# Both branch projections as seven products per block, with their operands and their merge passed through DRAM

## The reference

```
merged = jax.nn.sigmoid(ga_raw) * jnp.einsum('bne,ed->bnd', y_a, w_pa) + jax.nn.sigmoid(gb_raw) * jnp.einsum('bne,ed->bnd', y_b, w_pb)
return jnp.einsum('bnd,de->bne', merged, w_out)
```

## Time and profile before

| | |
|---|---|
| median of 3 runs | 1795.55 us (1794.21 to 1795.87) |
| the profiled execution's own time | 1793.51 us |
| its span, first to last instruction | 1791.8 us |
| PE busy | 98% |
| DVE busy | 59% |
| ACT busy | 34% |
| granted PE clock, mean | 0.996 of full speed |
| gate stage | from 692.0 to 844.4 us |
| branch stage | to 1018.5 us |
| output stage, first half of its columns | to 1064.8 us |

### The profile page before, as it was taken

How to read it: one execution, slowest core, us unless ns; L and a number is a source line. 1 busy time by engine, 2 the same in 40 slices (tenths; PEclk the granted TensorE clock), 3 DMA queues, 4 the chain that set the end, 5 groups by cost and what they waited for, 6 DMA issues and landing times.

```text
span 1791.8 us, 22991 instructions
## 1 busy us (share of the span) xinstructions
PE 1751.6 (98%) x8577; PEld 1471.9 (82%) x8577; DVE 1062.6 (59%) x1587; ACT 602.0 (34%) x937; POOL 169.2 (9%) x212
## 2 busy tenths in 40 slices
PE   6899999999999999999999999999999999999997
PEld 3698988989898888888888878888888888888886
DVE  4677636465557757456323546865656656566667
ACT  6534241423224324445210213533433333221112
POOL 1002020200112001111100100000000001222210
PEclk9999999999999999999999999999999999999999
DMA  7211111202078114334633433032222222722212
GB/s 308 71 49 35 60 48 48 69 23 71 19 239 295 48 71 137 122 100 150 230 95 94 140 107 141 24 118 71 85 79 70 96 91 70 284 103 94 94 47 95
DMA packets 100130, 187.75 MB, mean 105 GB/s; under 512 B 5810, under 2 KB 74562, under 8 KB 95714
## 3 DMA queue, kind: packets, MB, share of 16 engines
q1 hardware_dynamic: 83906, 130.11, 21.5%
q0 software_dynamic: 16160, 56.77, 8.9%
HBM read 150.11 MB, written 36.75 MB: 104 GB/s over the span
## 4 chain that ended last, share of the span: by engine, by line
PE 92%; DVE 4%; ACT 1%; DMA 1%; issue 1%; DVEq 0%; SPq 0%; ACTq 0%
PE PD L2126 23%; PE PM L2564 11%; PE PD L2564 11%; PE PD L2584 7%; PE PM L2584 6%; PE PD L2425 4%; PE PM L2425 4%; PE PD L2466 4%; PE PD L2236 4%; PE PD L2142 4%; PE PM L2309 2%; PE PM L2497 1%; PE PD L2249 1%; PE PD L2497 1%; PE PM L2402 1%
## 5 line engine op out<-in xcount | busy, mean ns | idle before, releaser
L2126 PE MATMUL PD<-R_hi,whi 128*128 128x512 f32 x480 | 149.5, 393 | 0.0
L2126 PE MATMUL PD<-R_lo,whi 128*128 128x512 f32 x480 | 148.1, 390 | 0.0
L2126 PE MATMUL PD<-R_hi,wlo 128*128 128x512 f32 x480 | 147.9, 389 | 0.0
L874 POOL TENSOR_TENSOR w_raw<-w_raw,g2B 128x2048 f32<-128x2048 f32 x11 | 50.9, 4626 | 651.1 <-DMA w_raw<-in_w_ff 487.2
L2126 PEld LDWEIGHTS PD<-R_hi,wlo 128*128 128x128 f32 x480 | 90.1, 188 | 19.1
L2126 PEld LDWEIGHTS PD<-R_lo,whi 128*128 128x128 f32 x480 | 90.1, 188 | 19.0
L2126 PEld LDWEIGHTS PD<-R_hi,whi 128*128 128x128 f32 x480 | 89.2, 188 | 17.9 <-issue 0.2
L901 ACT ACTIVATE whi<-raw 128x1024 fp32r<-128x1024 f32 x56 | 56.6, 1051 | 137.7 <-PE PD L2126 124.4
L1909 DVE TENSOR_TENSOR ws_lo<-S,ws_hi 128x512 fp32r<-128x512 f32 x76 | 56.3, 742 | 77.2 <-ACT ws_hi L1253 77.2
L2142 PE MATMUL PD<-whi,R_hi 128*128 128x256 f32 x256 | 72.8, 284 | 0.8 <-ACT vaug L967 0.8
L2142 PE MATMUL PD<-wlo,R_hi 128*128 128x256 f32 x256 | 72.4, 283 | 0.0
(11 more groups left out here) (495 smaller groups left out, 4607.6 us busy)
## 6 DMA issues: line engine op xcount, KB each, us to landing
rawF<-in_w_ff SPq DMA_DIRECT2D x44, 512.0 KB, 5.0
ada<-in_w_ada POOLq DMA_DIRECT2D x32, 512.0 KB, 5.3
raw<-in_w_in SPq DMA_DIRECT2D x30, 512.0 KB, 4.6
f_dram<-Fo SPq DMA_DIRECT2D x11, 1024.0 KB, 4.8
w_raw<-in_w_ff SPq DMA_DIRECT2D x11, 1024.0 KB, 5.0
f_raw<-f_dram SPq DMA_DIRECT2D x11, 1024.0 KB, 7.0
ada_raw<-in_w_ada SPq DMA_DIRECT2D x8, 1024.0 KB, 19.2
rawG<-in_w_in SPq DMA_DIRECT2D x16, 512.0 KB, 4.9
```

Of the source, the lines that this page charges most:

```text
L2126: i = mm(dst[:, e * HALF:e * HALF + width], wk[:, k, :], part, start=(k == 0 and step == 0), stop=(k == KT - 1 and step == 2))
```

## The change

The eight branch blocks are made by `gate_products` as well, as blocks 8 to 15 (`GATES` = 8, `GB` = 16): 8 to 11 for `y_a` with `w_pa`, 12 to 15 for `y_b` with `w_pb`. For this:

- Before the seven places can hold `y_a` or `y_b`, their sums must exist. `branch_sums` makes them on DVE in eight turns, two in each of the gate blocks 0 to 3; SP loads 1 MB into `y_ring` and stores 1 MB to `yT_dram` in each turn (`sums_load`, `sums_turn`).
- In blocks 7 and 11 (`FILL`) and the block after each, the places are refilled in 14 half places, as block 7 or 11 leaves them: SP loads half a place (512 KB) into one of four slots of `y_ring` (`place_load`), ACT splits it (`branch_hi`), DVE subtracts (`branch_lo`), and only then is the slot loaded again. In block 8 or 12 product n waits for its two halves (`branch_ready`).
- The merge works on quarters of 128x512 (`merge`): DVE multiplies with the gate in `g_ring`; for `y_a` POOL stores the result over the gate in `g_dram`, for `y_b` DVE adds what `m_ring` brought back.
- The split of the merged rows, the first two blocks of `w_out` (`wo_first`, `output_hi`, `output_lo`) and the loads of `x` move to block 15 and behind it.

```diff
+GATES, GB = 8, 16
+FILL = (GATES - 1, GATES + 3)
+            def sums_turn(u):
+                sp.wait_ge(branch_ready, u + 1)
+                sp.dma_start(yT_dram[:, u // KH, :, u % KH, :], y_ring[:, 1, :, :]).then_inc(sums_out, 16)
+                if u + 1 < UNITS:
+                    sums_load(u + 1)
...
             gate_block(0)
+            sp.wait_ge(yb_out, 16 * KT)
+            sp.wait_ge(mod_io, 32)
+            sp.wait_ge(sv_done, KT + 2)
+            sp.wait_ge(spill, 16 * HEADS + 1)
+            sums_load(0)
             sp.wait_ge(right_ready, 4)
             gate_block(1)
...
+            def branch_hi(fill, part):
+                j, at = fill * 2 * PRODUCTS + part, slice(part % 2 * 2, part % 2 * 2 + 2)
+                act.wait_ge(place_in[j % 4], 16 * (j // 4 + 2))
+                act.wait_ge(product, FILL[fill] * PRODUCTS + part // 2 + 1)
+                nc.scalar.activation(gate_right_hi[part // 2][:, at, :], ring_slot(j), ACT.Copy).then_inc(branch_hi_d, 1)
...
+            HI_AFTER = {0: (0, 1), 1: (2, 3), 3: (4, 5), 4: (6,), 5: (7,), 6: (8,)}
+            HI_LATER = {0: (9,), 1: (10, 11), 2: (12,), 3: (13,)}
...
+            def branch_sums(u):
+                dve.wait_ge(sums_in, 16 * (u + 2))
+                dve.wait_ge(sums_out, 16 * (u + 1))
+                own.link(v.tensor_tensor(y_ring[:, 1, 0:4:2, :], y_ring[:, 0, 1:4:2, :], y_ring[:, 0, 0:2, :],
+                                         ALU.subtract))
+                own.link(v.tensor_tensor(t2, t3, b11, ALU.add))
+                v.tensor_tensor(t4, b21, t2, ALU.subtract).then_inc(branch_ready, 1)
...
+            LO_AFTER = {1: (0, 1), 2: (2, 3), 4: (4, 5), 5: (6,), 6: (7,)}
+            LO_LATER = {0: (8, 9), 1: (10,), 2: (11, 12), 3: (13,)}
...
+                    if fill is not None:
+                        pe.wait_ge(branch_ready, UNITS + fill * 2 * PRODUCTS + 2 * n + 2)
...
-            with pe.Fori(0, 2) as i:
-                for hh in range(2):
-                    for m in range(2):
-                        pe.wait_ge(slot_free[m], i * 2 + (T_P1 // 2 + hh + 1))
-                        channels(m, i * 2 + (N_P1 + hh), hh, m, branch_hi, branch_lo,
...
+            for fill in range(2):
+                for q in range(2):
+                    for par in range(2):
+                        gate_products(GATES // 2 + 2 * fill + q, par, fill=fill if q + par == 0 else None)
...
             for b in range(2):
-                out_part(b)
-            out_tile(0, 1, range(KT - 1))
+                for t in range(3):
+                    out_part(b, t)
+            out_tile(0, 3, range(KT - 1))
```

More of the change, by code:

```diff
@@ new lines, in output_hi @@
+            def output_hi(b):
+                act.wait_ge(rawF_in[b], RAW_F)
+                if b == 0:
+                    act.wait_ge(product, (GB - 1) * PRODUCTS + 3)
+                else:
+                    act.wait_ge(merged, 2 * QUADS)
+                for half in range(2):
+                    at = slice(KH * half, KH * half + KH)
+                    nc.scalar.activation(wo_first[:, b, 0, half * 4 * CW:(half + 1) * 4 * CW],
+                                         rawG[b][:, at, :].rearrange("p k n -> p (k n)"), ACT.Copy)\
+                        .then_inc(pl_hi_d, 1)
@@ L1196, in m_hi @@
[L1196 to L1209, removed]
+                    if b in FILL:
+                        for part in HI_AFTER.get(n, ()):
+                            branch_hi(FILL.index(b), part)
@@ new lines, in _ @@
+                    if b - 1 in FILL:
+                        for part in HI_LATER.get(n, ()):
+                            branch_hi(FILL.index(b - 1), part)
+                    if b in (GB - 3, GB - 2) and n < 4:
+                        m_move(b - 1, n)
+                    if last:
+                        for part in M_HI_AFTER.get(n, ()):
+                            m_hi(part)
+                        if n == 3:
+                            output_hi(0)
+            m_hi(7)
+            output_hi(1)
@@ L1210, in _ @@
+            for part in range(8, len(M_FILL)):
+                m_hi(part)
+            act.wait_ge(m_ready, len(M_FILL))
             for n in range(2):
@@ new lines, in _ @@
+                    if b in FILL:
+                        for part in LO_AFTER.get(n, ()):
+                            branch_lo(FILL.index(b), part)
+                    if b - 1 in FILL:
+                        for part in LO_LATER.get(n, ()):
+                            branch_lo(FILL.index(b - 1), part)
+                    if last:
+                        if n < 6:
+                            for part in M_LO_AFTER.get(n, ()):
+                                m_lo(part)
+                        if n == 4:
+                            output_lo(0)
@@ L1867, in _ @@
+            for part in M_LO_AFTER[6]:
+                m_lo(part)
+            m_lo(7)
+            output_lo(1)
+            for part in range(8, len(M_FILL)):
+                m_lo(part)
+            dve.wait_ge(mod_io, 48)
+            g1B = g2B
             v.scalar_tensor_tensor(out=a2[:, :], in0=mod[:, 4, :], scalar=1.0, in1=cols[:, 24:32],
```

402 lines of the change are left out of this document (209 added, 193 removed).

## The result

| | before | after |
|---|---|---|
| median of 5 runs | 1795.55 us (1794.21 to 1796.52) | 1803.77 us (1801.4 to 1804.73) |
| the profiled execution's own time, its span | 1793.51, 1791.8 us | 1801.4, 1799.7 us |
| the sixteen blocks end at | 1018.5 us | 1028.70 us |
| second half of the output columns starts at | 1065.0 us | 1072.9 us |
| granted PE clock, mean | 0.996 | 0.99 |

The changed kernel is slower: ratio 1.0044 [1.0029, 1.0058], 8.2 us by the medians and 7.9 us by the spans. The prediction, 1788.7 us with 1779 to 1801, was wrong in sign and missed the range. The 7.9 us are all there by the middle of the output stage (1072.92 less 1065.03; the 1064.8 given ahead for the kernel before is the start of the last matmul ahead of this place). Only 0.5 us of them stand ahead of the first gate block, so the loss lies in the stages that the change touches.

What follows compares the result with a forecast made beforehand. PE, busy 98% of the span, was taken to bound the kernel. Savings of 21.8 and 2.4 us against added waits summed to -6.8 us, 1786.7 from the profiled execution, 1788.7 by the median; range 1779 to 1801.

Steps and rivals of the forecast that it cites:

- 96 matmuls fewer: Branch stage: eight blocks of 96 matmuls become eight of 84, 21.8 us less.
- wait at the output stage, 256-column tiles: Output stage: PE's 2.4 us wait for DVE's residual goes; 84 matmuls of 256 columns replace 42 of 512, +0.5 us.
- first wait: Gate stage's start: PE waits for block 0's second snapshot, behind y_b stores, sums load and block 1's weights; +8.0 us.
- clock behind it: After the gate stage's first wait PE runs at half clock for 3.1 us, half lost: +1.6 us; bounds 0 and 3.2.
- eight turns: Blocks 0 to 4: turns of 10.1 us, two per 19.04 us block, put DVE 1.1 us behind each block; +0.3 us.
- refills: Blocks 8, 11 and 12: DVE's list makes half places late, +3.0 and +4.0 us; bounds for the two 3 and 12.
- The third rival, slower: Gate blocks: weights queued ahead of a turn's transfers put DVE 3.8 us behind a block; net +4 to +5, 1800 us; chance 0.16.

Runs made afterwards that it cites:

- r_after: The changed kernel run once more, unaltered: 1802.31 us, ratio 1.0039 to the kernel before.
- e1_order: Changed kernel with SP loading block 1's weights before it waits for the y_b stores and loads the first operand of the sums: 1795.25 us, ratio 0.9998.
- e8_quarter: e4_all with only a quarter of each half place loaded, copies and subtractions at full size: 1775.57 us, ratio 0.9888.
- e2_place: Changed kernel with SP's loads of half places 12 and 13 put ahead of the weights of the block after next: 1794.99 us, ratio 1.0002.
- e6_snap_all: e4_all with ACT's copies of half places 10 to 13 put behind the snapshots in blocks 8 and 12: 1777.73 us, ratio 0.9903.
- e10_light: e6_snap_all with DVE's subtraction of each half place cut to 256 of 1024 columns, loads whole: 1770.2 us, ratio 0.9864.
- e3_spread: Changed kernel with the eight turns of the sums spread over blocks 0 to 5 instead of 0 to 3: 1797.93 us, ratio 1.0016.
- e5_late: Changed kernel with SP's loads of half places 14 to 17 issued one block later: 1802.53 us, ratio 1.0037.
- e4_all: Changed kernel with the edits of e1_order, e2_place and e3_spread together: 1780.31 us, ratio 0.9917.

## Why the prediction was wrong

The sum, term by term, by the profiled executions:

| term | predicted | `after` | `r_after` |
|---|---|---|---|
| 96 matmuls fewer | -21.8 | -21.8 | -21.8 |
| wait at the output stage, 256-column tiles | -1.9 | -2.3 | -2.3 |
| first wait | +8.0 | +9.7 | +9.6 |
| clock behind it | +1.6 | +3.0 | +1.6 |
| eight turns | +0.3 | +2.6 | +4.6 |
| refills | +7.0 | +16.1 | +14.2 |
| gate stage begins later | 0 | +0.5 | +1.3 |
| sum | -6.8 | +7.8 | +7.2 |

- **The saving was right.** Undisturbed blocks take 19.04 us; block 15's end is -21.8 + 9.7 + 3.0 + 2.6 + 16.1 + 0.5 = +10.1 us late, where 10.2 are read (1028.70 against 1018.5), and the output stage gives 2.3 back: its first 126 matmuls take 15.11 us for the forecast 15.1, and the 2.4 us wait of the earlier trace rows is not there.
- **The first wait was right in mechanism and 1.7 us short**, inside its bounds of 5.6 to 11.7. The load went out at 701.52 (forecast 701.4). The weights landed at 711.4 instead of 709.0: 8.48 us after their issue, behind the load for the sums, and not the 7.0 of the earlier trace rows.
- **The clock was right within its bounds.** 5.9 us at half speed in `after`, near the upper bound of 3.2 us lost, and 3.2 us in `r_after`, just as forecast, behind a wait of the same length (9.7 and 9.6 us). One profile could not have given the size of this term. That the clock would fall behind the shorter waits in the refills, and behind the turns in some executions, was not in the sum.
- **The turns failed by their size.** "A turn [...] is 10.1 us": seven turns take the 75.6 us from 717.28 to 792.87, 10.8 each. The chain divides it: 7.66 us of transfers in the mean (7.00 to 8.53) for 7.5, 2.64 of DVE for 2.57, and 0.43 between DVE's last step and the load's issue (717.28 to 717.71), in which SP issues the store, and which I had left out. The text itself said that the case decides at 10.2. By its own schedule, counted from the late start of block 1 and so with the cover of the first wait in it, turns of 10.8 us would have cost some 4.7 us (an estimate: 715.0 and seven times 10.8, plus the 3.9 us of steps, against 13.6 us into its block 4 at 776.2). Block 1 started 5.2 us later than in that schedule (724.27 for 719.1), and the first turn ended 2.3 us later (717.28 for 715.0), so the cover was larger and 2.6 us came of it; in e1_order, without cover, 9.4. The third rival, slower, named this place, but neither its condition (a turn over 11 us in the mean) nor its 11 us came about in the changed kernel.
- **The refills failed by the most, 9.1 us (7.2 in `r_after`).** The step was "about 1.4 us of waiting, because half place 12 is loaded behind the weights of block 10 in SP's list". The timeline at that place of the changed kernel:

```profile
862.71 2.67 SPq L630 DMA_DIRECT2D y_ring<-yT_dram  x2
...
865.43 0.98 SPq L598 DMA_DIRECT2D rawG<-in_w_pa  x2
...
868.11 1.47 SPq L630 DMA_DIRECT2D y_ring<-yT_dram  x2
...
877.37 1.06 ACT L1246 ACTIVATE R_hi<-y_ring 128x1024 fp32r<-128x1024 f32 x1 [4.37 <-DMA y_ring<-yT_dram]
878.33 0.58 ACT L1232 ACTIVATE snapG<-PD 128x512 f32<-128x512 f32 x1
879.05 0.47 PE L2545 MATMUL PD<-G_hi,gw_hi 128*128 128x512 f32 x1 [3.45 <-ACT snapG L1232]
```

The half place lands 9.2 us after its issue, behind two other half places and 1 MB of weights, 2 MB in all that SP had issued since 862.71 us. What the core moves in the meantime:

```profile
868.11:877.34 9.23, 6.06 (x26) 4.40 (x24) 5.97 (x7) 2.63 (x4) 1.52 (x3) 1.00 1.02 391
```

That is 3.6 MB by 391 GB/s, for a load of half a MB. I had seen the order and given it 1.4 us; my upper bound for it (7 us a time, 12 in all) was too low too. Its second effect was not in the sum at all: ACT's copy waits for it in order, and the snapshot that PE needs sooner stands behind. The third is the clock, at 0.50 again from 880 us after a wait of 3.45 us.

How the 16.1 us divide: e8_quarter puts DVE's list at 6.0 us, close to the 7.0 of the sum (which held 1.4 us of waiting too). So the step that failed is the 1.4 us for the queue and what hangs on it. The other 10 are loads, the snapshots behind them and the clock; e2_place takes nearly 8 of them out by SP's order alone (8.2 us are left in the two blocks). What stays after all the edits is DVE: e6_snap_all with 6.8 us and e10_light with none, on the same loads. What e6_snap_all loses above e8_quarter, 0.8 us, was not followed further; the two are not quite alike, since e8_quarter keeps ACT's old order and has one wait of 1.0 us for a snapshot. Nor was it followed why e1_order and e3_spread spread over 9 to 10 us from run to run.

The Trainium skill's page DMA: Bandwidth & Descriptors (section Specifications), cited with about 358 GB/s for a core, would have made the turns 0.8 us longer, and they are 0.7 longer. The trace does not agree with the reason: the windows below pass that figure (404 to 424 GB/s, on one core alone), and most of the 0.7 is the issue. The changed kernel while ACT waits for the half place:

```profile
874.00:875.00 1.00, 1.00 (x7) 0.80 (x6) 0.85 (x1) 0.00 (x0) 0.00 (x0) 1.00 1.04 424
...
877.00:878.00 1.00, 0.00 (x0) 0.00 (x0) 0.00 (x0) 0.63 (x1) 0.00 (x0) 1.00 1.05 404
```

## What to carry to other kernels

A transfer's duration from a quiet stretch is not its landing time behind others: add up the bytes that its own queue and the other ones still hold and get meanwhile (3.6 MB here), divide by what a full slice moves, and put the load that is wanted first ahead in the list (here 7 to 8 us for four issues moved). On an engine that works in order, look for the instruction that others wait for and what stands ahead of it: a copy for a later product that waits for a DMA makes the snapshot for the next product late. Stalls in a row hide each other, so a repair of one shows mostly the next: order and spread gained 7 to 8 and 4 to 5 us alone and 16 together, and the same saving that was 8 us slower with three stalls was 18 us faster without most of them.

## What the runs showed of the hardware

- Half place 12, a load of 512 KB behind 2 MB of other loads of the same queue, took 9.2 us from issue to use (868.11 to 877.34), 7.6 in r_after and 9.8 in e5_late, while the core moved 391, 369 and 336 GB/s. The median over the sixteen loads of this kind, by the page of `after`, is 5.5 us, so the median tells nothing of the one that counts.
- A wait of PE of 9.7 us was followed by 5.9 us at half clock (3.0 us lost), and in r_after one of 9.6 us by 3.2 us; after a wait of 2.5 us it had been 3.1 us. Waits of 2.2 to 2.3 us in a busy stretch went both ways: full clock behind them in `after`, half for 3.4 us in r_after and e1_order. A wait of 3.45 us, three us behind one of 1.4, was followed by half clock too. So the length of one wait does not give what the clock costs behind it. The 7.7 us that e4_all loses in block 12 are this, whole: 5.1 us of waiting, and then half clock from 940.0 to 945.1 us, 2.5 us lost. Its windows there:

```profile
940.00:942.00 2.00, 1.96 (x5) 1.62 (x6) 1.55 (x2) 2.00 (x4) 0.00 (x0) 0.50 1.09 376
942.00:944.00 2.00, 2.00 (x6) 1.56 (x5) 2.00 (x3) 1.31 (x2) 0.00 (x0) 0.50 0.81 291
944.00:946.00 2.00, 2.00 (x8) 1.63 (x7) 1.93 (x4) 0.58 (x1) 0.00 (x0) 0.72 0.07 25
```
